# Modulation weights on the four column quarters of the array, unsplit; retention values centred in other places

## What is computed

```python
def adaln(cvec, w, b):
    m = jax.nn.silu(cvec) @ w + b
    return jnp.split(m[:, None, :], N_MOD, axis=-1)
...
px = modulate(rms_norm(x, norm_mix[i]), sh1, sc1) @ w_in[i]
pc = modulate(rms_norm(xc, norm_mix[i]), csh1, csc1) @ w_in[i]
```

```python
y = yf + yb                                    # rwkv_mix, heads of 64
mu = jnp.mean(y, axis=-1, keepdims=True)
y = (y - mu) * lax.rsqrt(var + GN_EPS) * ln_w + ln_b
...
o = (inner + cross).reshape(B, S, H, Dh)       # retention, heads of 128
mu = jnp.mean(o, axis=-1, keepdims=True)
```

## Time and profile before

| | us |
|---|---|
| median of 3 runs | 3165.48 |
| lowest and highest | 3152.08, 3172.03 |
| the profiled execution | 3176.06 |
| its span, first to last instruction | 3174.3 |
| mean granted TensorE clock | 0.991 |

### The profile page before, as it was taken

One profiled execution on the slowest core, in us unless ns is written; L12 is line 12 of the kernel. 1 busy time (PEld: TensorE's weight loads), 2 busy tenths in 40 slices (PEclk: granted clock), 3 DMA queues, 4 the chain that ended last, 5 costly groups with the idle time before them and its releaser, 6 DMA issues.

```text
span 3174.3 us, 62635 instructions
## 1 busy us (share of the span) xinstructions
PE 3072.8 (97%) x26939; PEld 2651.8 (84%) x26939; DVE 2100.7 (66%) x2893; ACT 1571.4 (50%) x2161; POOL 245.6 (8%) x307
## 2 busy tenths in 40 slices
PE   6799999999999998999999999999999999999998
PEld 4578888888888887888888888888878888888887
DVE  5776656767787867555555556679986666665554
ACT  5555545565665644444444434456644444444333
POOL 1000000023332310000000000012200000000000
PEclk9899999999999999999999999999999999999999
DMA  9667766820000034666666565665545555665564
GB/s 335 201 212 245 244 223 212 253 82 8 11 9 8 8 104 152 199 186 186 186 186 187 178 196 179 218 177 160 156 154 184 186 186 186 186 186 187 185 188 143
DMA packets 549246, 529.56 MB, mean 167 GB/s; under 512 B 16916, under 2 KB 545706, under 8 KB 548074
## 3 DMA queue, kind: packets, MB, share of 16 engines
q1 hardware_dynamic: 546074, 516.08, 52.1%
q0 software_dynamic: 2832, 9.45, 0.9%
q10 hardware_dynamic: 64, 0.02, 0.0%
HBM read 521.28 MB, written 4.19 MB: 166 GB/s over the span
## 4 chain that ended last, share of the span: by engine, by line
PE 86%; DVE 9%; ACT 2%; DMA 2%; issue 1%; POOL 0%; DVEq 0%; ACTq 0%; POOLq 0%
PE ps L2003 39%; PE ps L2004 19%; PE ps L2134 10%; DVE lo L1216 3%; PE ps L2013 2%; PE ps L2042 2%; PE ps L2014 2%; PE ps L2015 2%; PE ps L2043 2%; PE ps L2396 1%; PE ps L2157 1%; PE ps L2144 1%; PE ps L2142 1%; ACT hi L800 1%; PE ps L2397 1%
## 5 line engine op out<-in xcount | busy, mean ns | idle before, releaser
L1216 DVE TENSOR_TENSOR lo<-raw,hi 128x1024 fp32r<-128x1024 f32 x936 | 1137.6, 1235 | 654.0 <-ACT hi L800 651.1
L800 ACT ACTIVATE hi<-raw 128x1024 fp32r<-128x1024 f32 x936 | 972.5, 1055 | 829.3 <-PE ps L2004 594.1
L2003 PE MATMUL ps<-mov,hi 128*128 128x512 f32 x3680 | 1303.3, 399 | 6.0 <-DVE mov L1278 4.8
L2004 PE MATMUL ps<-mov,lo 128*128 128x256 f32 x3680 | 1032.7, 281 | 0.0
L2003 PEld LDWEIGHTS ps<-mov,hi 128*128 128x128 f32 x3680 | 691.9, 188 | 180.8 <-issue 6.3
L2004 PEld LDWEIGHTS ps<-mov,lo 128*128 128x128 f32 x3680 | 695.4, 189 | 0.1
L2003 PE MATMUL ps<-hid,hi 128*128 128x512 f32 x704 | 248.8, 399 | 0.0
L2042 PE MATMUL ps<-hi,c 128*32 128x256 f32 x768 | 190.6, 288 | 40.2 <-DVE lo L1216 40.0
L820 ACT ACTIVATE tmp<-ps 128x512 f32<-128x512 f32 x157 | 93.8, 597 | 269.8 <-PE ps L2004 263.1
L2004 PE MATMUL ps<-hid,lo 128*128 128x256 f32 x704 | 197.7, 281 | 0.0
L2043 PE MATMUL ps<-lo,c 128*32 128x256 f32 x768 | 187.5, 284 | 0.0
(11 more groups left out here) (373 smaller groups left out, 4148.5 us busy)
## 6 DMA issues: line engine op xcount, KB each, us to landing
raw<-in_w_in SPq DMA_DIRECT2D x184, 512.0 KB, 4.6
raw<-in_w_mod SPq DMA_DIRECT2D x160, 512.0 KB, 4.9
raw<-in_w_gate SPq DMA_DIRECT2D x88, 512.0 KB, 4.5
raw<-in_w_up SPq DMA_DIRECT2D x88, 512.0 KB, 4.4
raw<-in_w_down SPq DMA_DIRECT2D x88, 512.0 KB, 4.6
raw<-in_w_ffn_gate SPq DMA_DIRECT2D x88, 512.0 KB, 4.6
raw<-in_w_ffn_up SPq DMA_DIRECT2D x88, 512.0 KB, 4.5
raw<-in_w_ffn_down SPq DMA_DIRECT2D x88, 512.0 KB, 4.3
```

The source lines that it names most:

```text
L800: act.activation(hi[:, s, :, :], src, ACT.Copy).then_inc(hi_ready, 1)
L1216: dve.tensor_tensor(lo[:, s, :, :], raw_at(ph, i, j)[0], hi[:, s, :, :].bitcast(F32), ALU.subtract)\
L2003: pe.matmul(ps[:, b, :], hi[:, s, kk, w], moving(k, None), start=first, stop=False)
L2004: mm = pe.matmul(ps[:, b, 0:T], lo[:, s, kk, w], moving(k, 0), start=False, stop=last)
```

## The change

- **Unsplit modulation chunks.** `mod_rows` multiplies the raw chunk in fp32 by `c4` read as fp32: row block kk goes to array columns and `ps` partitions 32 kk to 32 kk + 31. One product for each row block in place of two. No `hi` and `lo` for these 192 chunks. `mrow` and `mrow2` take 128 partitions, and `sel` adds the parts of all four quarters.
- **Own buffers.** A planner (`all_chunks`) lays out every chunk: in `in_kv` and `in_rest` the main chunks use the 4 raw buffers and two halves of `hi` and `lo`, and the side chunks 4 buffers of their own, which lie in the other two halves (`spare`). A side buffer is free when TensorE is done with its last chunk.
- **Order.** The side chunks come before a main chunk, evenly: three sides and one main in `in_kv`, one and one in `in_rest`. `in_kv` looks 4 chunks ahead, and its first main chunk is split before the phase, behind the first two operand groups.
- **Centred values in the scan.** The value rows are turned by `less_mean64` (identity less 1/64) in place of the identity, and the mean's product and subtraction go. One wait of TensorE moves from level 2 to level 4.
- **Retention.** TensorE reads the head's values where they lie; POOL's copy goes, and TensorE waits for `bank_free` instead.

```diff
             for c in self.rows_order:
-                self.order.append((False, p, c))
                 per = SIDES.get(name, 0) // pairs
-                if c < per:
-                    self.order += [(True, per * p + c, e) for e in range(n)]
+                self.order += [(True, per * p + t // n, t % n) for t in range(per * c, per * c + per)] + [(False, p, c)]
...
-    sel[0, 0] = sel[1, 0] = sel[2, 1] = sel[3, 1] = 1
+    for first in range(0, P, 32):
+        sel[first:first + 2, 0] = 1
+        sel[first + 2:first + 4, 1] = 1
...
-    lookahead = lambda ph: 2 if ph.name in EARLY else 3
+    lookahead = lambda ph: 4 if ph.name == "in_kv" else 2 if ph.name in EARLY else 3
...
+    def all_chunks():
+        out, in_buffer, in_half = [], {}, {}
+        mains = sides = splits = paired = 0
+        for ph in order:
+            for j in list(range(ph.chunks)) * ph.trips:
+                g, whole, mixed = len(out), ph.whole(j), ph.name in SIDES
+                if ph.name == "mod":
+                    buffer = g % (2 * RING)
+                else:
+                    buffer = RING + sides % RING if whole else mains % RING
+                    sides, mains = sides + whole, mains + (not whole)
+                half, half_free, used = 0, 0, []
+                if not whole:
+                    half = paired % 2 if mixed else splits % RING
+                    paired, splits, used = paired + mixed, splits + 1, [half]
+                elif mixed:
+                    used = [2 + buffer % 2]
+                raw_free = None
+                if buffer in in_buffer:
+                    last, load = in_buffer[buffer]
+                    raw_free = (split_free, last + 1 + SPLIT_CREDIT) if out[last].whole else (lo_ready, out[last].split)
...
-                        if ph.name != "mod":
-                            sp.wait_ge(lo_ready, ph.chunk(i, j) + 1)
-                        elif j >= 2 * RING:
-                            sp.wait_ge(lo_ready, j - 2 * RING + 1 + RING)
+                        if chunks[ph.chunk(i, j)].raw_free:
+                            sp.wait_ge(*chunks[ph.chunk(i, j)].raw_free)
...
-                retg.done(pool.tensor_copy(rv[:, :], one(p2, h + RV)), "v")
...
+            split(PH["in_kv"], 0, 3)
             gemm(PH["in_kv"], shift_both, first_groups)
...
-                if stage == "c":
-                    gnp.wait(dve, "mean", b)
-                    gnd.done(dve.scalar_tensor_tensor(out=y, in0=ps[:, bank, 0:T], scalar=-1.0 / HEAD, in1=y, op0=ALU.mult, op1=ALU.add), "c")
...
-                        pe.wait_ge(lo_ready, ph.chunk(i, j) + (1 + RING))
+                        if ph.whole(j):
+                            src, arrived, loads = raw_at(ph, i, j)
+                            pe.wait_ge(arrived, loads * 16)
+                        else:
+                            pe.wait_ge(lo_ready, chunks[ph.chunk(i, j)].split)
...
-            def mod_rows(b, s, kk, k, first, last):
-
-                pe.matmul(ps[0:32, b, 0:CN], c4[:, k, :], hi[:, s, kk, :], start=first, stop=False)
-                return pe.matmul(ps[0:32, b, 0:CN], c4[:, k, :], lo[:, s, kk, :], start=False, stop=last)
+            def mod_rows(b, src, c):
+
+                for kk in range(CK):
+                    cols = slice(32 * kk, 32 * kk + 32)
+                    mm = pe.matmul(ps[cols, b, 0:CN], c4[:, c * CK + kk, :].bitcast(F32), src[:, kk, :], start=(c == 0), stop=(c == KB // CK - 1))
+                return mm
...
-                if stage == 2:
-                    gnp.done(pe.matmul(ps[:, bank, 0:T], blk64, ymix[:, ds(b, 1), :], start=True, stop=True), "mean")
...
-                each(scan_pe[0], 0, (q, "tV"), 2, lambda c, hs: stV[hs, c, :], None, off=T)
+                each(scan_pe[0], 0, (q, "tV"), 2, lambda c, hs: stV[hs, c, :], lambda c, hs: less_mean64[hs, :], off=T)
...
-                    retg.wait(pe, "v", h)
+                    pe.wait_ge(bank_free, trip_out(h))
                     for n in range(2):
-                        mm = pe.matmul(ps[:, 7, n * P:(n + 1) * P], rv[:, n * P:(n + 1) * P], less_mean, start=True, stop=True)
+                        mm = pe.matmul(ps[:, 7, n * P:(n + 1) * P], one(p2, h + RV)[:, n * P:(n + 1) * P], less_mean, start=True, stop=True)
```

More of the change, by code:

```diff
@@ L8 @@
+import dataclasses
 from contextlib import ExitStack
@@ L105, in completed, with whole @@
         return (side, p) if c == self.last_rows(side) else None
+    def whole(self, j):
+        return self.name == "mod" or (j < self.chunks and self.order[j][0])
     def last_rows(self, side):
@@ new lines, in program @@
+    class Chunk:
+        whole: bool
+        buffer: int
+        load: int
+        split: int
+        half: int
+        raw_free: tuple
+        half_free: int
+    def all_chunks():
[20 more added lines that the diff above has]
+                else:
+                    load = 0
+                in_buffer[buffer] = (g, load + 1)
+                for n in used:
+                    if not whole and n in in_half:
+                        half_free = in_half[n] + 1 + SPLIT_CREDIT
+                    if whole and n in in_half and not out[in_half[n]].whole:
+                        pe_done = in_half[n] + 1 + SPLIT_CREDIT
+                        raw_free = (split_free, max(pe_done, raw_free[1] if raw_free and raw_free[0] is split_free else 0))
+                    in_half[n] = g
+                out.append(Chunk(whole, buffer, load + 1, splits, half, raw_free, half_free))
+        return out
@@ L602, in load_vectors @@
+    chunks = all_chunks()
+    def raw_at(ph, i, j):
+        c = chunks[ph.chunk(i, j)]
+        n = c.buffer - RING
+        if n < 0:
+            tile = raw[:, c.buffer, :, :]
+        elif ph.chunk(i, j) < PH["in_kv"].g0:
+            tile = raw_more[:, n, :, :]
+        else:
+            tile = spare[n // 2][:, n % 2, :, :]
+        return tile, raw_in[c.buffer], c.load
     def load_vectors(eng, which):
@@ L790, in _ @@
             chain = Chain(act, a_chain)
+            split_done = set()
             def split(ph, i, j):
[L794 removed]
+                g = ph.chunk(i, j)
+                if g >= TOTAL or chunks[g].whole or g in split_done:
                     return
[L796 removed]
+                split_done.add(g)
+                s = chunks[g].half
                 src, arrived, loads = raw_at(ph, i, j)
                 act.wait_ge(arrived, loads * 16)
[L799 removed]
+                if chunks[g].half_free:
+                    act.wait_ge(split_free, chunks[g].half_free)
                 act.activation(hi[:, s, :, :], src, ACT.Copy).then_inc(hi_ready, 1)
@@ L1211, in split @@
             def split(ph, i, j):
-                if isinstance(i, int) and ph.chunk(i, j) >= TOTAL:
+                g = ph.chunk(i, j)
+                if g >= TOTAL or chunks[g].whole or g in split_done:
                     return
-                s = ph.slot(j)
-                dve.wait_ge(hi_ready, ph.chunk(i, j) + 1)
+                split_done.add(g)
+                s = chunks[g].half
+                dve.wait_ge(hi_ready, chunks[g].split)
                 dve.tensor_tensor(lo[:, s, :, :], raw_at(ph, i, j)[0], hi[:, s, :, :].bitcast(F32), ALU.subtract)\
@@ L1979, in trip @@
                             pe.wait_ge(bank_free, ph.pair(i, p) + 1)
-                        pe.wait_ge(lo_ready, ph.chunk(i, j) + (1 + RING))
+                        if ph.whole(j):
+                            src, arrived, loads = raw_at(ph, i, j)
+                            pe.wait_ge(arrived, loads * 16)
+                        else:
+                            pe.wait_ge(lo_ready, chunks[ph.chunk(i, j)].split)
                         if ready and p == 0 and not side:
                             pe.wait_ge(*ready(c))
-                        for kk in range(CK if not chunk else 0):
+                        if ph.whole(j):
+                            mm = mod_rows(4 + 2 * (p % 2) if side else ph.bank(p), src, c)
+                        for kk in range(CK if not (chunk or ph.whole(j)) else 0):
                             k = c * CK + kk
[L1985 to L1990, removed]
+                            if ready_block and i == 0 and p == 0:
+                                pe.wait_ge(*ready_block(k))
+                            mm = product(p, chunks[ph.chunk(i, j)].half, kk, k, k == 0, k == last)
                         if chunk:
-                            mm = chunk(p, ph.slot(j), c)
+                            mm = chunk(p, chunks[ph.chunk(i, j)].half, c)
                         mm.then_inc(split_free, 1)
@@ L2315, in last_norm @@
             def last_norm(i, j):
-                if i == 0 and j == 0:
-                    for e in range(2):
-                        scan_y[e].wait(pe, "y", RB - 1)
-                    group_norm(RB - 1, 2, bank=5)
                 if i == 0 and j == 1:
```

47 lines of the change are left out of this document (19 added, 28 removed).

## The result

The changed kernel takes **3130.2 us** (median of 4 runs, 3120.06 to 3139.05) against 3158.78 of the kernel before, measured beside it (4 runs, 3145.86 to 3172.03): ratio 0.990, 95% interval 0.986 to 0.993. Beside later experiments it took 3123.48 against 3148.03, ratio 0.990 again. It is faster by about 1%, a quarter of the 108 us that the sum promised, and 0.2 us outside the range. The two profiled executions differ by more, 39.9 us, since that of the kernel before was a long one (3176.06, above all four runs).

A forecast was written before the change was run, and what follows sets the result against it. TensorE, busy 97% of the span, was taken to bound the kernel. Savings of 25 + 4 + 45 + 21 + 4 + 9 = 108 us off the median of 3165.5 gave 3058 us, with a range of 3035 to 3130.

The forecast's parts named there:

- Price of a chunk: Modulation chunk on TensorE: four column quarters run at once, 0.44 us in place of 0.94.
- rival A: Modulation chunks: only pairs of products overlap (0.87 us), or all share one stream (0.94); 3122 us; chance 0.18.
- C: Modulation chunks: quarters of the same rows run one after the other, 1.73 us a chunk; slower, 3258 us; chance 0.12.
- First phase: 64 modulation chunks before the first projection come at the DMA's pace; 25 us saved.
- Sides of `in_kv`: 96 modulation chunks between the main chunks of `in_kv`, where TensorE is full, each give 0.50 us; 45 us saved.
- Start of `in_kv`: First pairs of `in_kv`: VectorE's side splits go, 6 us of stall regained, 2 lost to the main chunk's split; 4 saved.
- rival B: In `in_kv`, a main chunk's load waits behind two sides in SP's queue; 22 us lost, 3080 us; chance 0.15.
- Half the lack counts: Groups of `in_kv`: one group's stall gives slack to the next, leaving 0.5 to 0.9 us more per group.
- `in_rest`: 32 modulation chunks in `in_rest` give 16 us, own buffers and even order 5 more; 21 us saved.
- Scan: Seven scan blocks lose one product of 256 columns on TensorE's full queue; 4 us saved.
- retention: In the heads, TensorE no longer waits for POOL's copy; 9 of 10.9 us of waits saved.
- Rival D: Price as in rival A; first phase gives nothing, as TensorE, idle between DMAs, falls to half clock; 3142 us; chance 0.05.

The follow-up runs named there:

- e8: The changed kernel with a modulation chunk's four products on two column quarters in turn, not four; 3168.95 us in one run.
- e3: The changed kernel with all four products of a modulation chunk on one column quarter; 3275.8 us, ratio 1.037 to the kernel before.
- e5: The changed kernel with main chunks loaded two groups earlier and the selecting product behind the next main chunk; 3052.21 us, ratio 0.966 to the kernel before.
- e1: The changed kernel with main chunks' loads issued one group earlier in `in_kv` and `in_rest`; 3073.44 us, ratio 0.972 to the kernel before.
- e9: The changed kernel, load order kept, with a finished side's selecting product behind the next main chunk; 3098.64 us, ratio 0.983 to the kernel before.
- e2: The changed kernel with main chunks' loads issued two groups earlier in `in_kv` and `in_rest`; 3062.72 us, ratio 0.969 to the kernel before.
- e6: The changed kernel, unsplit quarters and own buffers kept, with the chunk order of the kernel before; 3100.74 us, ratio 0.981 to the kernel before.
- e4: The changed kernel with unsplit quarters in the first phase only, sides of `in_kv` and `in_rest` as before; 3113.79 us, ratio 0.987 to the kernel before.
- e7: The kernel before with only the centring product in the scan and retention's values read in place; 3149.62 us, ratio 0.9964.
- e10: The changed kernel once more, unaltered, run and profiled again; 3123.48 us.

## Why the prediction was wrong

**Price of a chunk: right.** 0.44 us, and 0.87 and 1.73 with fewer quarters (e8, e3). Rivals A and C fall as to their price. The 3122 of rival A is nearest to the measured time, but by luck: its price did not occur. In after, the four first records of a chunk start within 21 ns and the four second ones 0.24 us later, on four column quarters with the same rows. The Trainium skill (TensorE: Matmul & The Clock Gate, Part 3: Packing small matmuls) says that weight loads overlap running products only where row groups differ, and that products keep program order. The prediction worked out 0.87 us a chunk from it; the measured 0.44 decides against that for this case.

**First phase: right.** The chunks come at the DMA's pace (share 1.07) although the granted clock was 0.81 there. 122.1 us against "near 126".

**Sides of `in_kv`: the step that failed**, and with it "Start of `in_kv`". The saving of TensorE's time was sized rightly: in e5, where no main chunk is late, a pair falls by 5.7 us (35.2 to 29.5), and 45 over eight pairs is 5.6. (That the whole stage falls by 48.3 against 4 + 45 = 49 is partly luck: the first pair gave 13.3 and the last with `in_lora` 0.5, where 9.6 and 5.6 were counted.) But I let the sum stand on a TensorE that never waits for a main chunk, and gave the wait to rival B, with 22 us and a chance of 0.15. Its mechanism, the main chunk's load behind two sides in SyncE's queue, is what happened (e1 removes it by order alone, and the stage falls from 324.9 to 273.1), and its sign, TensorE idle before the main chunks, is there; its size was off. I had the main chunk ready 9.7 us after the group's sides began. Measured, its products can start 12.2 after (241.48 to 253.64):

| term | forecast, us | measured, us |
|---|---|---|
| until the load is issued | 0.9 | 1.66 |
| from issue to landing | 6.5 | 7.24 |
| `hi` and `lo` | 2.3 | 2.3 |
| row copy and selecting product behind `lo` | not counted | 0.9 |

The measured column is the group of the timeline above. "Half the lack counts" was sound. If a main chunk can start L after the sides of the group before it, and the next sides start 5.7 later, two groups have gone by: a group settles at (L + 5.7)/2 = 8.95 us. Pairs two to seven measured 36.0 on average (35.2 in the second profile), 9.0 a group, against 7.4 forecast (the terms given there add up to 7.3). Over 32 groups that is about 50 us. The left-out 0.9 is 14 of them by this rule, and e9 agrees for the middle pairs. Rival B's own price has a slip: half of its lack of 1.0 is 0.5 a group, 16 us; for the 0.7 that it used it gives no row.

Against the 263 us forecast (312 less 49) the stage took 62 more: 38 in pairs two to seven, 9 in the first pair, 14 in the last with `in_lora`. Of the 14, the stall at the end of the stage is 4.0, and the lower clock behind it about 3; the prediction has no term for either. Of the 9 in the first pair, a stretch of the lower clock from 144.8 us on adds 2.4 to one main chunk; the rest is not worked out. The granted clock has a part in the 38, too, that I can't take apart from the lateness. TensorE, stalled, falls to its lower level, 1.2 GHz: in after in six stretches of 3 to 7 us between 209 and 428 us, such as the third window above (0.51 of 2.4 GHz). Each begins during an idle time of TensorE of 1.6 to 4.0 us or up to 2 us behind it. Five main chunks of `in_kv` take 6.9 to 7.8 us in them and not 5.3, 10 us in all at most. In e1, e2 and e5 the same stage has one such stretch behind 130 us, and it begins within the 4.0 us stall at the end.

**Start of `in_kv`: nothing, and not 4.** The first pair lasts 43.3 against 43.6, where its sides alone should have given 5.6 and the start 4 more. The gain shows only when the main chunks come in time: 33.5 in e1, 30.3 in e5.

**`in_rest`: mis-sized.** 10.7 in place of 21; e5 shows 15.0. ScalarE's waits for `w_in` are gone but for one of 9.4, as forecast. They had cost little: TensorE was idle for only 6.5 of the 193.7 us of `in_r` and `in_rest` before, and for 2.8 in e5, so own buffers gave 3.7 and not 5. TensorE's busy time fell by 11.3 (187.2 to 175.9) and not 16. An estimate of the rest: a side that stands alone takes 0.57 from its start to that of the main chunk (244.55 to 245.12), 0.13 over its price, and there are 32 such places now and were 8, which is 3 us. After itself lost 4 more: TensorE is idle for 3.2 us before the first main chunk of `in_rest`, and within that falls to the lower clock for 6.8; e1 has neither.

**Scan, retention: right in kind.** 3.0 for 4, 6.7 for 9. In the range, the parts of the forecast's own range (17 less, 30 more) give 3041 to 3088 and not 3039 to 3090; nothing hangs on it. **Rival D** named idle TensorE at the lower clock as the danger, but in the first phase; there it cost nothing that shows, and in `in_kv` it did.

## What to carry to other kernels

Unsplit products with 32 stationary columns cost a quarter on four column quarters of what they cost on one, even if they share all rows. (Split products on four quarters were not tried.) Shortening an engine's work is not enough where its data comes in one queue behind transfers that wait for that engine: work out, for each load, when the queue reaches it, and issue the load with the longest preparation behind it (landing and splits, here 10 us) a group ahead. Here that took no further buffer and gave 57 to 67 us of 3130 in the medians (e1, e2), and 54 to 57 in the two stages that it touches. What stands behind a late instruction on its engine (here a row copy behind a split) is late with it, and its waiter too. And look at the ends of a stage: a buffer scheme that is right within it cost 4 us at its border here.

## What the runs showed of the hardware

Four unsplit f32 products on four column quarters, with the same rows of the array, run side by side: 0.44 us for four, 0.87 with two quarters, 1.73 with one. A main chunk's load of 512 KB took 4.7 us to land in the median of after, 7.2 as the last of three issued within 1.0 us (after), and 9.5 as the last of five issued within 2.1 us (e6).

Projections of stages that no edit touches came at two paces at the full clock. Busy time from 2400 to 2500 us, first the kernel before, then e5:

```profile
2400.00:2500.00 100.00, 100.00 (x566) 86.75 (x565) 64.85 (x73) 46.99 (x55) 0.00 (x0) 1.00 0.60 184
```

```profile
2400.00:2500.00 100.00, 100.00 (x579) 88.19 (x578) 62.33 (x65) 47.29 (x54) 0.00 (x0) 1.00 0.61 190
```

566 records in 100 us against 579, 2% at the same clock of 1.00. The stages from `out_2` on take 862 to 865 us at the one pace (before, both profiles of after, e3, e8) and 848 or 849 at the other (e1, e2, e4 to e7, e9); `ffn` takes 500 or 491, and e1, e6 and e7 have the slow pace in `ffn` and the fast one at the end. In the slow one, the step from a record with `hi` to the next with `lo` is uneven (0.232, 0.236, 0.241), in the fast one even (0.230 at all of e5's from 2400 to 2500 us). So up to 27 us of a span, 0.9%, are not the edit's; the stage table above is free of it, since both of its kernels had the slow pace. Whether the pace belongs to the execution or to how the kernel enters the stage is not shown, but the runs point to the execution: 17 executions of the unchanged kernel before, beside e5, spread from 3145.39 to 3176.28, 31 us, and the profiled executions with both stages slow lie at or near the top of their kernel's runs (3176.06, 3132.05 in e10), those with both fast at or near the bottom (3043.16 in e5, 3083.47 in e9).
